# Output projection of a hybrid decoder layer: the residual's transposes of a unit moved together to the unit's opening

## The reference

```python
mixed = jnp.concatenate([rmsnorm(o_attn, g_attn_out), rmsnorm(o_conv, g_conv_out)], axis=-1)
x = x + mixed @ w_o
hm = rmsnorm(x, g_mlp_norm)
x = x + jnp.square(jax.nn.relu(hm @ w_up)) @ w_down
```

## Time and profile before

| | |
|---|---|
| median of 3 runs | 1413.86 us (1413.68 to 1415.95) |
| profiled execution, first to last instruction | 1409.7 us |
| median above that span | 4.2 us |
| PE busy, share of the span | 93% |
| DVE, ACT, POOL busy | 51%, 29%, 14% |
| TensorE clock granted, mean | 0.980 |

### The profile page before, as it was taken

How to read it: one execution, slowest core, us unless ns; L and a number is a source line. 1 busy time by engine, 2 the same in 40 slices (tenths; PEclk the granted TensorE clock), 3 DMA queues, 4 the chain that set the end, 5 groups by cost and what they waited for, 6 DMA issues and landing times.

```text
span 1409.7 us, 21751 instructions
## 1 busy us (share of the span) xinstructions
PE 1315.8 (93%) x8348; PEld 1298.5 (92%) x8348; DVE 716.3 (51%) x1271; ACT 401.9 (29%) x801; POOL 199.2 (14%) x216
## 2 busy tenths in 40 slices
PE   3899988997958889999999999999999999999997
PEld 2899877897958889999999999999999999999997
DVE  6302757677575446435445344354453544587342
ACT  5332445455434222102111011121110211254232
POOL 6623434434130000000000000000000000041000
PEclk9999999999989899999999999999999999999999
DMA  5521011001103221321111111111111111111221
GB/s 153 131 60 32 1 48 30 16 16 35 46 17 75 62 65 41 77 52 45 48 47 54 45 45 45 45 45 45 45 45 45 45 50 39 46 45 54 69 68 46
DMA packets 111132, 70.99 MB, mean 50 GB/s; under 512 B 3226, under 2 KB 109622, under 8 KB 111064
## 3 DMA queue, kind: packets, MB, share of 16 engines
q1 hardware_dynamic: 110584, 68.37, 17.7%
q0 software_dynamic: 480, 1.93, 0.5%
q10 hardware_dynamic: 16, 0.00, 0.0%
HBM read 65.69 MB, written 5.54 MB: 51 GB/s over the span
## 4 chain that ended last, share of the span: by engine, by line
PE 77%; DVE 8%; ACT 4%; issue 4%; DMA 3%; POOL 2%; SPq 1%; DVEq 0%; ACTq 0%
PE acc L1534 71%; PE aux L1549 3%; DMA x_col<-in_x_sample 2%; DVE prob L1265 2%; PE aux L1534 1%; POOL act_lo L669 1%; DVE conv L1365 1%; POOL sq_sum L793 1%; DMA w_st<-in_w_in 1%; PE aux L1682 1%; DVE ropea L1218 1%; DVE o_tok L1305 1%; ACT sq_new L1097 1%; DVE pt_lo L1281 1%; ACT w_hi L805 0%
## 5 line engine op out<-in xcount | busy, mean ns | idle before, releaser
L1534 PE MATMUL acc<-xg_hi,w_hi 128*128 128x352 f32 x960 | 312.0, 325 | 0.0
L1534 PE MATMUL acc<-xg_lo,w_hi 128*128 128x352 f32 x960 | 307.8, 321 | 0.0
L1534 PE MATMUL acc<-xg_hi,w_lo 128*128 128x352 f32 x960 | 307.7, 321 | 0.0
L1534 PE MATMUL acc<-a_hi,w_hi 128*128 128x352 f32 x768 | 247.7, 323 | 0.0
L1534 PE MATMUL acc<-a_lo,w_hi 128*128 128x352 f32 x768 | 246.1, 320 | 0.0
L1534 PE MATMUL acc<-a_hi,w_lo 128*128 128x352 f32 x768 | 245.9, 320 | 0.0
L1534 PE MATMUL acc<-act_hi,w_hi 128*128 128x352 f32 x624 | 215.1, 345 | 13.2 <-issue 12.8
L1534 PE MATMUL acc<-act_hi,w_lo 128*128 128x352 f32 x624 | 208.3, 334 | 0.0
L1534 PE MATMUL acc<-act_lo,w_hi 128*128 128x352 f32 x624 | 208.2, 334 | 0.0
L1449 DVE TENSOR_TENSOR xt<-acc,xt 128x352 f32<-128x352 f32 x192 | 100.3, 522 | 179.1 <-PE acc L1534 178.1
L805 ACT ACTIVATE w_hi<-w_st 128x1024 fp32r<-128x1024 f32 x98 | 102.9, 1050 | 280.0 <-PE acc L1534 273.8
(11 more groups left out here) (199 smaller groups left out, 1598.6 us busy)
## 6 DMA issues: line engine op xcount, KB each, us to landing
w_st<-in_w_up SPq DMA_DIRECT2D x32, 512.0 KB, 4.1
w_st<-in_w_down SPq DMA_DIRECT2D x32, 512.0 KB, 3.4
w_st<-in_w_in SPq DMA_DIRECT2D x18, 512.0 KB, 3.9
w_st<-in_w_o SPq DMA_DIRECT2D x8, 512.0 KB, 4.6
w_st<-in_w_ple_gate SPq DMA_DIRECT2D x8, 512.0 KB, 4.3
x_nat<-in_x_prompt SPq DMA_DIRECT2D x11, 352.0 KB
x_col<-in_x_prompt SPq DMA_DIRECT2D x8, 484.0 KB
out<-y_col SPq DMA_DIRECT2D x8, 484.0 KB
```

Of the source, the lines that this page charges most:

```text
L1534: ins_ = pe.matmul(out, w[a][cols], x[b][tile_], start=(k == 0 and p == 0), stop=(k == len(terms) - 1 and p == 2))
```

## The change

A unit first turns all three chunks of the residual and then has its three products. The wait for the unit's weights moves behind the transposes.

```diff
             def out_units(i, first):
                 for s in range(2):
-                    pe.wait_ge(wlo_ready, 2 * i + (U_OUT + s + 1))
                     pe.wait_ge(xcol_landed, 96 * i + 48 * (s + 1))
                     for c in range(NCH):
                         pe.wait_ge(aux_free[c], 2 * i + (OUT_USE[c] + s))
                         turn(aux[c], [((every, slice(k * XT, (k + 1) * XT)), x_col[0:XT, XPC * c + k, :])
                                       for k in range(XPC)]).then_inc(x_turned, 1)
+                    pe.wait_ge(wlo_ready, 2 * i + (U_OUT + s + 1))
+                    for c in range(NCH):
                         pe.wait_ge(att_lo, c + 1)
                         pe.wait_ge(mix_lo, c + 1)
                         pe.wait_ge(acc_free[c], 2 * i + (U_OUT + s))
```

## The result

The changed kernel takes 1391.08 us (median of 4 runs, 1389.12 to 1394.09); the kernel before beside it took 1414.90 (1413.68 to 1416.46). The ratio is 0.9836, 95% interval 0.9814 to 0.9858. The forecast was 1390.8 with a range of 1388.0 to 1396.0. The span of the profiled execution went from 1409.7 to 1387.3 us, the mean granted clock from 0.980 to 0.984.

A forecast was written before the change was run, and what follows sets the result against it. PE's products bound the kernel, with stands for the late residual transfer in the output projection. Units 1 to 7 at 87.6 instead of 110.72 us give span 1386.6, plus 4.2 makes 1390.8 us; range 1388.0 to 1396.0.

The forecast's parts named there:

- The bound and the price: Output projection: PE stands 6 times, 14.2 us in all, for the late residual transfer, with slower products behind five waits.
- The sum: Units 1 to 7: 12.6 plus six of 12.5, so 87.6 us in place of 110.72, 23.1 less.
- five slow products: Products right behind PE's waits for the residual, partly at the low clock; 1.4 to 1.6 us each to be saved.
- The 4.2 us between span and median: Amount by which the runs' median stands above the profiled span, added to the span of 1386.6.
- A unit by itself: Output projection unit without waits: twelve transposes 0.95 us and three products 11.55, together 12.5, the same as before.
- The load: Residual block issued about 1.0 us after a unit opens, usable at 7.1 of 12.5 us; margin 5.4 us.
- What is late next: A unit's third turn needs the bank ACT frees: covered by 1.9 us, except in unit 1, which takes 12.6.
- took the transfer's place: Rival at the unit openings: a late ACT copy of chunk 2 holds all three products; 1426.5 us, chance 2%.
- Unit 0, the step that was mis-sized: First product waits for the tail's bank, starting near 405.2; release of chunk 2 unmoved; price 0, bounds 0 and +0.9.
- The rule on transposes: Skill's rule that transposes don't engage the full rate, so grouping invites the low clock at every opening; sum kept against it.
- The rival with 1402.0: Low clock behind twelve transposes: units 1 to 7 each open with a product at 5.43, costing 11.2 us; chance 4%.

The follow-up runs named there:

- The filled wait: The kernel before, with 15 unused matmuls added ahead of PE's wait for the residual in units 2 to 7; 1407.01 us, ratio 0.9941.
- the standing filled: The kernel before with the residual reloaded by chunk, plus unused matmuls ahead of unit 0's three products; 1388.48 us, ratio 0.9817.

## Why the prediction was right

**The bound and the price.** It was the reload's issue. Holding it back alone brought back the whole time and the same list of waits; issuing it early alone gave the whole gain. The sum had 23.1 us: 14.2 of standing, five slow products at 1.4 to 1.6, and the rest behind the waits. The seven units gave 23.7. The filled wait splits the loss into 6.6 to 8.5 for the clock and 15 to 17 for standing, so both terms had roughly the right size.

**The last digit.** That the medians agree with the forecast within 0.3 us is partly luck. The span was put at 1386.6 and came to 1387.3: 0.6 more in unit 0 and 0.6 of scatter ahead of it, 0.5 less in units 1 to 7. The 4.2 us between span and median were taken as fixed and came to 3.8. The traced execution took 1389.12, 1.8 above its own span, and was the fastest of its four; the rest of that term depends on which execution the trace caught.

**A unit by itself.** Put at 12.5, measured 12.40; unit 1 put at 12.6, measured 12.69; together 87.6 against 87.06. "The move itself is worth nothing" was a little short: the run that reloads by chunk has a turn ahead of each product and takes 87.4, so grouping gives 0.3 to 0.6 us over seven units.

**The load.** The margin was put at 5.4 us. The held reloads bracket it: with the issue 3.8 us later than in the changed kernel there is no wait; with it 7.5 us later PE waits six times, 14.5 us in all. That is 2.4 us each, which makes the margin 5.1 us by this estimate. The weights follow the block by 3.0 us (441.54, 444.52), as worked out.

**What is late next.** ACT's copy of chunk 2 was the next in line, and only for unit 1. The timeline of ACT in the changed kernel:

```profile
404.87 0.57 ACT L1027 ACTIVATE tail_tok<-aux 18x512 f32<-18x512 f32 x1
...
411.98 0.55 ACT L968 ACTIVATE root_c<-aux,eps 128x352 f32<-128x352 f32 x1 [0.47 <-PE aux L1695]
...
427.94 0.45 ACT L1043 ACTIVATE xt<-aux 128x352 f32<-128x352 f32 x1
...
438.19 0.45 ACT L1043 ACTIVATE xt<-aux 128x352 f32<-128x352 f32 x1
```

The copy for unit 0 ends at 428.39 and the third turn of unit 1 stands behind it at 428.43; for unit 1 it ends at 438.64, 1.65 us ahead of the unit's end at 440.29, against 1.9 put. The bank never took the transfer's place.

**Unit 0, the step that was mis-sized.** It had price 0, bounds 0 and 0.9; the traces show 0.6 (0.4 to 0.5 between the longer ones of the last section). The root slipped as worked out (its idle of 0.47 behind the late sum, L1695) and DVE's reciprocal did not wait for it. What the text left out is that ACT's split of the attention half stands behind that root, and POOL's (L752) behind ACT: it slipped too, into DVE's four operations of L1320, and the release of chunk 2 hangs on those. The Trainium skill, "SBUF — State Buffer", section Who interferes with whom, says that a DVE instruction with two inputs from SBUF contends with a GpSimd instruction that reads SBUF. The traces agree: L1320 reads `conv` and `root_c`, and 0.58 us more of overlap cost 0.59.

**The rule on transposes.** Twelve transposes opened each of units 1 to 7, seven times within 87 us, and the granted clock stayed at 1.00, with three products behind them in 11.48. These are 0.91 us of transposes at a time between products, and 1.89 us in the row of 24; what a longer stretch of nothing but transposes would do, no run here shows. The rival with 1402.0 has no trace of itself.

## What to carry to other kernels

A buffer that exists once is loaded when its last reader lets go of it, so the reader's place in the order sets the start of the transfer: either move all readers to the front of the work that covers the load, or let the load follow the readers piece by piece. Both gave the same 23 us here, and once the block landed before the opening, an earlier issue was worth nothing more. When TensorE stands for a late transfer, price the product behind it as well: here about a third of the loss was the low clock, and it could be bought back even with the transfer still late.

## What the runs showed beyond this

Unit 0's products behind a stand have no fixed length. The same changed kernel opened unit 1 after 30.04 us in one profiled execution and after 31.96 in another (columns as in the tables above):

```profile
397.56:427.60 30.04, 17.30 (x89) 16.06 (x88) 23.46 (x31) 11.79 (x16) 8.48 (x5) 0.83 0.15 35
```

```profile
398.78:430.74 31.96, 19.24 (x88) 18.00 (x87) 24.75 (x33) 12.54 (x17) 8.46 (x5) 0.73 0.14 35
```

The granted clock is 0.83 in one and 0.73 in the other. In the second the first product took 6.3 us instead of 5.1, so the sum behind it came late enough to hold DVE's reciprocal by 0.57 us, and POOL's split ran 0.5 us more beside L1320. The third product took longer as well, 6.2 us instead of 5.5 from its start to unit 1's opening. With the standing filled, at a granted clock of 1.00, these two products took 3.85 and 4.06. A spread of 2 us between runs of one kernel can thus come from the clock of two products; why it falls one way or the other in an execution was not tried.

The order of before shows the same two lengths in five traces, three times 29.5 and twice 31.6. The changed order has the longer one in four of its five, 31.96 to 32.08. Whether the order of unit 0 also makes the longer one more frequent, so few traces cannot tell.
